# Channel layer norm of the convolution branch: block sums on VectorE ahead of one all-ones product, in place of eight products

## The reference, cut to what matters

```
a = a_val * sigmoid(a_glu)
y = depthwise_conv(a, width 31) + conv_b
mu = mean(y over the 1024 channels)
yc = y - mu
y = yc * rsqrt(mean(yc * yc over the 1024 channels) + eps) * cln_g + cln_b
ya = silu(y) * silu(a_z)
yb = windowed_attention(q, k, v) * silu(b_z)
h = h + concat(ya, yb) @ w_out
```

## Time and profile before

| | |
|---|---|
| median of three runs | 2235.05 us |
| profiled execution, first to last instruction (span) | 2231.8 us |
| TensorE matmul busy | 2197.3 us (98%) |
| TensorE weight load busy | 1929.3 us (86%) |
| VectorE busy | 1695.6 us (76%) |
| ScalarE busy | 1071.7 us (48%) |
| GpSimd busy | 546.4 us (24%) |
| mean granted TensorE clock | 0.998 |

### The profile page before, as it was taken

The page is one execution under the profiler, slowest core; times in us unless marked ns, Lnnn a source line. Parts: engine busy times, 40 slices in busy tenths (PEclk is TensorE's granted clock), DMA queues, the critical chain, the costliest instruction groups (busy, mean ns, idle before and its releaser), DMA issues.

```text
span 2231.8 us, 38880 instructions
## 1 busy us (share of the span) xinstructions
PE 2197.3 (98%) x14626; PEld 1929.3 (86%) x14626; DVE 1695.6 (76%) x2875; ACT 1071.7 (48%) x1429; POOL 546.4 (24%) x225
## 2 busy tenths in 40 slices
PE   7999999999999999999999999999999999999997
PEld 6888888888888888899999887888888888888886
DVE  7688678885888588788888666788888884447887
ACT  5445464445454464555554644444444443334454
POOL 4676641017767530110001322200000000000001
PEclk9999999999999999999999999999999999999999
DMA  7454445555554445554445300555555555555554
GB/s 254 169 181 169 155 170 179 188 185 197 177 181 165 144 178 187 187 193 166 165 157 194 114 3 21 192 186 188 187 188 188 188 188 188 188 188 189 188 209 168
DMA packets 69320, 384.89 MB, mean 172 GB/s; under 512 B 15120, under 2 KB 23056, under 8 KB 24272
## 3 DMA queue, kind: packets, MB, share of 16 engines
q1 hardware_dynamic: 69200, 383.22, 48.8%
HBM read 380.02 MB, written 3.18 MB: 172 GB/s over the span
## 4 chain that ended last, share of the span: by engine, by line
PE 92%; DVE 4%; ACT 1%; DMA 1%; issue 1%; POOL 0%; SPq 0%; DVEq 0%; POOLq 0%; ACTq 0%
PE ps L259 47%; PE ps L260 25%; PE ps L262 3%; PE ps L247 3%; PE ps L249 2%; PE ps L248 2%; PE ps L886 1%; DVE low L234 1%; PE ps L867 1%; DMA raw<-weights_dram 1%; PE ps L875 1%; PE ps L1882 1%; PE ps L1934 0%; PE ps L1926 0%; ACT whi L229 0%
## 5 line engine op out<-in xcount | busy, mean ns | idle before, releaser
L259 PE MATMUL ps<-opA,whi 128*128 128x512 f32 x2460 | 871.9, 395 | 0.3 <-DVE low L234 0.3
L260 PE MATMUL ps<-opA,low 128*128 128x256 f32 x2624 | 706.7, 279 | 0.2 <-DVE opA L1004 0.2
L229 ACT ACTIVATE whi<-raw 128x2048 fp32r<-128x2048 f32 x346 | 660.2, 1909 | 77.4 <-DMA raw<-weights_dram 76.2
L234 DVE TENSOR_TENSOR low<-raw,whi 128x2048 fp32r<-128x2048 f32 x252 | 583.3, 2315 | 67.8 <-ACT whi L229 52.2
L259 PEld LDWEIGHTS ps<-opA,whi 128*128 128x128 f32 x2460 | 461.0, 187 | 106.2 <-issue 2.8
L241 POOL TENSOR_TENSOR low<-raw,whi 128x2048 fp32r<-128x2048 f32 x95 | 436.6, 4606 | 433.6 <-ACT whi L229 407.2
L259 PE MATMUL ps<-opB,whi 128*128 128x512 f32 x1380 | 494.5, 398 | 14.9 <-DVE opB L418 12.1
L260 PEld LDWEIGHTS ps<-opA,low 128*128 128x128 f32 x2624 | 492.0, 188 | 14.3 <-DVE opA L1004 0.5
L260 PE MATMUL ps<-opB,low 128*128 128x256 f32 x1472 | 397.3, 280 | 0.0
L259 PEld LDWEIGHTS ps<-opB,whi 128*128 128x128 f32 x1380 | 259.7, 188 | 78.1 <-DVE low L412 10.5
L268 ACT ACTIVATE crossed<-ps 128x256 f32<-128x256 f32 x168 | 64.6, 384 | 490.6 <-PE ps L262 490.4
(11 more groups left out here) (399 smaller groups left out, 2660.9 us busy)
## 6 DMA issues: line engine op xcount, KB each, us to landing
raw<-weights_dram SPq DMA_DIRECT2D x350, 1024.0 KB, 4.8
bias_t<-table_dram SPq DMA_DIRECT2D x16, 384.0 KB, 6.0
hT<-xT_dram SPq DMA_DIRECT2D x4, 512.0 KB, 9.0
out_dram<-hT SPq DMA_DIRECT2D x3, 512.0 KB, 2.8
lora_g<-lora_dram SPq DMA_DIRECT2D x1, 1024.0 KB, 5.1
p_in<-pT_dram SPq DMA_DIRECT2D x2, 256.0 KB, 5.2
lora_wa<-lora_dram SPq DMA_DIRECT2D x1, 512.0 KB, 5.5
chunk_mats_dram<-compact SPq DMA_DIRECT2D x4, 128.0 KB, 3.9
```

Source lines behind the costliest of these rows:

```text
L229: act.activation(whi[:, v % RING, :], raw[:, v % RING, :], ACT.Copy).then_inc(hi_done.sem, 1)
L234: v_.tensor_tensor(wlo(v % RING, 0, width), raw[:, v % RING, 0:width], whi[:, v % RING, 0:width].bitcast(F32), ALU.subtract).then_inc(lo_d ...
L259: pe.matmul(*cross, start=start, stop=False)
L260: mm = pe.matmul(ps[:, b, 0:T], wlo(s, w0, w0 + P), op[:, k, 0:T], start=False, stop=False)
```

## The change

The seven sums of y_ln's blocks, and three sums of y_sq (four blocks onto four, two onto two, one onto one), are done by VectorE; TensorE then does one all-ones product for the mean and one for the variance. y_sq grows to eight blocks and its second half now lies on bias_t, so ScalarE's second square waits until VectorE has read the last rows of bias_t (biased(8), in step 38), and both squares stand in step 38 ahead of ScalarE's gate(38). The sum y_sum takes p_in's place.

```diff
-        y_sq = place("y_sq", [P, 4, T], at=arena + 1088)
+        y_sq = place("y_sq", [P, 8, T], at=arena + 1088)
+        y_sum = place("y_sum", [P, T], at=arena + 11528)
...
                     if m == 38:
                         act.wait_ge(*fr["centred"](1))
-                        act.activation(y_sq[:, :, :], y_ln[:, 0:4, :], ACT.Square).then_inc(fr["y_sq"].sem, 1)
-                    if m == 39:
-                        act.wait_ge(*fr["var_mm"](1))
-                        act.activation(y_sq[:, :, :], y_ln[:, 4:8, :], ACT.Square).then_inc(fr["y_sq"].sem, 1)
+                        act.activation(y_sq[:, 0:4, :], y_ln[:, 0:4, :], ACT.Square).then_inc(fr["y_sq"].sem, 1)
+                        act.wait_ge(*fr["biased"](PAIRS))
+                        act.activation(y_sq[:, 4:8, :], y_ln[:, 4:8, :], ACT.Square).then_inc(fr["y_sq"].sem, 1)
...
                         else:
-                            ins = v.scalar_tensor_tensor(y_ln[:, cc, :], taps, w, y, ALU.mult, ALU.add)
-                            if cc == CB - 1:
-                                ins.then_inc(fr["conv"].sem, 1)
-                                v.wait_ge(*fr["conv"](1))
-                            else:
-                                link(ins)
+                            link(v.scalar_tensor_tensor(y_ln[:, cc, :], taps, w, y, ALU.mult, ALU.add))
+                            if cc:
+                                ins = v.tensor_tensor(y_sum[:, :], y_ln[:, 0, :] if cc == 1 else y_sum[:, :], y_ln[:, cc, :], ALU.add)
+                                if cc == CB - 1:
+                                    ins.then_inc(fr["y_sum"].sem, 1)
+                                else:
+                                    link(ins)
...
+                    if m == 38:
+                        v.wait_ge(*fr["y_sq"](2))
+                        for x in (4, 2):
+                            link(v.tensor_tensor(y_sq[:, 0:x, :], y_sq[:, 0:x, :], y_sq[:, x:2 * x, :], ALU.add))
+                        v.tensor_tensor(y_sq[:, 0, :], y_sq[:, 0, :], y_sq[:, 1, :], ALU.add).then_inc(fr["sq_sum"].sem, 1)
                     if m == 39:
-                        v.wait_ge(*fr["var_mm"](2))
+                        v.wait_ge(*fr["var_mm"](1))
...
-                def variance(x):
-                    pe.wait_ge(*fr["y_sq"](x + 1))
-                    for c in range(4):
-                        mm = pe.matmul(ps[:, 5, T:2 * T], ones[:, :], y_sq[:, c, :], start=x == 0 and c == 0, stop=x == 1 and c == 3)
-                    mm.then_inc(fr["var_mm"].sem, 1)
+                def variance():
+                    pe.wait_ge(*fr["sq_sum"](1))
+                    pe.matmul(ps[:, 5, T:2 * T], ones[:, :], y_sq[:, 0, :], start=True, stop=True).then_inc(fr["var_mm"].sem, 1)
...
                 def mean():
-                    pe.wait_ge(*fr["conv"](1))
-                    for c in range(CB):
-                        mm = pe.matmul(ps[:, 5, 0:T], ones[:, :], y_ln[:, c, :], start=c == 0, stop=c == CB - 1)
-                    mm.then_inc(fr["mean"].sem, 1)
+                    pe.wait_ge(*fr["y_sum"](1))
+                    pe.matmul(ps[:, 5, 0:T], ones[:, :], y_sum[:, :], start=True, stop=True).then_inc(fr["mean"].sem, 1)
...
-                    if m in (38, 39):
-                        variance(m - 38)
+                    if m == 39:
+                        variance()
```

More of the change, by code:

```diff
@@ L481, in program @@
         att_keysT = [place(f"keysT{x}", [P, KV_HEADS, T], at=area + x * KB * 2 * T + 8 * P) for x in range(2)]
-        fr_counts = {"flip_in": 16, "p_in": 16, "p_hi": 1, "p_lo": 1, "gate": 24, "gated": 24, "conv": 1,
+        fr_counts = {"flip_in": 16, "p_in": 16, "p_hi": 1, "p_lo": 1, "gate": 24, "gated": 24,
                      "tok": 1, "tok_read": 1, "turned": 1, "v_read": 1, "k_read": 1,
@@ L485, in program @@
                      "out": 8, "normed": 8, "outT": 8, "mixed": 8, "hi": 8, "lo": 8,
-                     "mean": 1, "centred": 1, "y_sq": 2, "var_mm": 2, "var": 1, "dev": 1, "inv": 1, "scaled": 1,
+                     "mean": 1, "centred": 1, "y_sq": 2, "y_sum": 1, "sq_sum": 1, "var_mm": 1, "var": 1, "dev": 1, "inv": 1, "scaled": 1,
                      "affine": 8, "th": 8, "once": 8, "w": 8, "w_hi": 8, "w_lo": 8,
```

## The result

| | before | after |
|---|---|---|
| median, same chip | 2234.91 us (4 runs) | **2265.35 us** (2262.70 to 2267.57, 4 runs) |
| profiled execution: span, own time | 2231.8 us | 2263.4 us, 2265.39 us |
| TensorE matmul, busy | 98% | 97% |
| VectorE busy | 1695.6 us | 1755.9 us |
| GpSimd busy | 546.4 us | 545.9 us |

The change makes the kernel slower: ratio 1.0137, 95% interval 1.0123 to 1.0150. That is 30.4 us more, where 21.2 were forecast. TensorE has 14 products fewer in each layer and yet lost.

What follows compares the result with a forecast made beforehand. TensorE was taken to set the front's pace; 8.6 us a layer, 17.2 for both, plus 4 us of clock on the 2231.8 us span gave 2253.0, and 3.25 us outside it 2256.3 us; 80% range 2240 to 2272.

Steps and rivals of the forecast that it cites:

- Products removed: Layer norm on TensorE: 14 of 16 all-ones products go, at 0.43 us each, 6.0 us a layer saved.
- The row that decides: VectorE beside GpSimd splits: a two-SBUF-input operation waits for the split's end; the engine that has waited is served next.
- blocked sum: VectorE block sum beside a GpSimd split: ends 0.28 us after the split, making VectorE 3.67 us late.
- GpSimd's keeping its turn: Rival, paired splits: the second split precedes the waiting sum, VectorE 8.2 us late, +27.3 us a layer, some 2311 us; 12%.
- the absence of blocking: Rival, sums beside splits: each costs its plain 0.42 us, -4.3 us a layer, 2226.4 us; 8%.
- Blocks 1 to 6: Block sums in the groups: 0.1 us for block 1, then 1.07 us in each of five groups, 5.35 us.
- The mean: Block 7's sum at step 35: held by a split, TensorE starts at 259.22 instead of 255.58, 3.64 us.
- The variance: Sums of squares: the split goes ahead of the third sum, TensorE waits 5.5 us; 1.2 us if unblocked.
- A layer in all: One layer's sum of terms: 0.1 + 5.35 + 3.64 + 5.5 - 6.0 = +8.6 us; +17.2 us for both.
- The clock: TensorE's clock after the mean and variance waits: one fall a layer at 2.0 us, +4 us, bounds 0 and 8.
- The 3.25 us outside the span: Outside first and last instruction: median of runs lies 3.25 us above the profiled span, where nothing changes.

Runs made afterwards that it cites:

- the products alone: Against the kernel before: one product for the mean, one for the variance, no VectorE sums, the other blocks left out of the computation; 2223.57 us (0.9949).
- fills: Changed kernel plus unread products in TensorE's waits: in groups, at mean and variance, 2260.37 us; at mean and variance only, 2257.65 us.
- the second experiment: Changed kernel with the three sums of squares replaced by one reduction over eight blocks, block sums as changed; 2255.73 us (1.0100 to the kernel before).
- the first experiment: Changed kernel with the running sum of the blocks kept in PSUM, sums of squares as changed; 2238.90 us (1.0023 to the kernel before).
- the third experiment: Changed kernel with both the running block sum in PSUM and one reduction for the squares; 2231.39 us (0.9993 to the kernel before).

## Why the forecast was right in sign and short in size

Step by step, by the forecast's own terms (layer 0 of the profiled execution, falls of the clock taken out):

- **Products removed, 6.0 us a layer:** right, 6.06 and 6.12 with the products alone.
- **The row that decides** (two SBUF inputs and a split exclude each other; the engine that waited is served): right. The forecast's blocked sum is 3.67 us, the median 3.672. GpSimd's keeping its turn did not happen in any of the twelve sums that had a second split behind the first (block 7 has none), and the absence of blocking in none of the fourteen.
- **Blocks 1 to 6:** 5.45 us forecast. From the start of the first group to that of the last block (83.75 to 250.19, before 83.84 to 242.77) it is 7.51 us; the one group with a fall has 6.89 us between two evictions where the others have 5.34, 1.55 us. Left: 5.96, as 1.15 us a group instead of 1.07 and 0.2 for block 1.
- **The mean:** 3.64 us forecast; 11.02 - 7.42 = 3.6 from the shifts of TensorE's product (255.58 to 266.60) and of L694 ahead of it (242.77 to 250.19).
- **The variance:** wait 5.5 us forecast, 5.25 measured; with fills 0.36.
- **A layer in all:** 8.6 us forecast. 15.35 - 1.55 - 4.9 = 8.9 in layer 0; in layer 1, where a group has a fall of about the same 1.55 us, 14.3 - 1.55 - 3.8 = 8.95. Both layers together 17.9 instead of 17.2.
- **The clock: the term that failed.** I counted one fall a layer at 2.0 us, 4 us, with 8 as the upper bound. Measured: three a layer, 1.55 + 4.9 and 1.55 + 3.8, 11.8 us in the fronts. One of the three falls behind a wait of 0.9 or 1.1 us in a group, which the forecast had priced at nothing. Placing a wait "nearer" to 1.60 or to 10.49 by its ratio was a guess between two rows, and the rows were too far apart to carry it: 3.5 us at the mean gave a fall in both layers here and in only one of two in the second experiment, and even 0.93 us gave one once. The 2.0 us for one fall was near: 1.9 to 2.45 us at the mean and the variance (half of what the two cost together), 1.55 in a group.
- **The 3.25 us outside the span** were 2.0: the profiled execution after has 2265.39 us for a span of 2263.4. The forecast took the distance between a median of other executions and this span for a constant, and so hid 1.3 us of its error.

Against the span the forecast was 2253.0 us and the measurement 2263.4: 10.4 us, of which 7.8 are the falls in the fronts (11.8 - 4), 0.7 the waits and products there, and 1.9 the net of what lies behind the fronts: 1.2 for the longer wait of the second block and 1.5 for the fall behind it, less 0.8 that came back ahead of it in places that were not traced. The forecast had nothing for that last part, and no edit touches it.

What stays open: why eight of the forty waits of about 1 us in the groups (two of ten in the changed kernel, and one, two and three of ten in the three others that have them unfilled) dropped the clock and the others didn't, and why the wait of the second block was 2.73 us here and 1.52 before. It ends on ScalarE's rounding, which waits there for a load of weights, and it comes out long or short in kernels with quite different fronts.

## What to carry to other kernels

Before work is moved to VectorE, look at what GpSimd does at that moment and at where the operands lie: with two SBUF inputs a 0.42 us addition takes up to the rest of GpSimd's instruction, here 3.7 us, and a PSUM operand or another moment makes it 0.42 us again. A reduction with one SBUF input ran beside a split unharmed, but not every one-input operation does: the one on sinT in the earlier trace rows was held for 4.75 us. Idle time of an engine covers such a delay only once a group, and the idle time that is left decides, not the mean busy share. And price each new wait of TensorE twice, once for itself and once for the clock: here the late sums cost 18 us beyond the 12 us of products that they saved, and the falls of the clock in the fronts 12 us more.

## What the runs showed of the hardware beyond that

- **An engine that has waited is served between two instructions of the other that stand back to back.** GpSimd's pair of splits took 9.32 us with a sum in the middle and 9.16 without, although the second split was ready; the other eleven such pairs took 9.30 or 9.31 us. At the variance it was GpSimd that had waited, and it went ahead of VectorE's third sum.
- **One wait, two outcomes.** The second block's wait, over all twelve kernels: seven had it at 1.40 to 1.99 us, with no window under 1.00 behind it; five at 2.73 to 2.94 us, each with a window at 0.66 to 0.79. At the start, 1.15 to 1.60 us left the clock alone, and 1.97 to 2.30 us brought it to 0.70 to 0.78 and cost 1.3 us. TensorE's timeline there in the first experiment, and the windows of the same kernel:

```profile
17.19 0.50 PE L259 MATMUL ps<-opB,whi 128*128 128x512 f32 x1 [2.02 <-DVE opB L418]
```

```profile
15.00:20.00 5.00, 2.98 (x11) 2.42 (x10) 4.91 (x9) 4.48 (x9) 0.00 (x0) 0.76 1.02 363
20.00:25.00 5.00, 5.00 (x27) 4.32 (x27) 4.85 (x4) 5.00 (x6) 0.00 (x0) 0.90 0.62 197
```

  Yet 1.99 us in one place had no fall and 1.97 us in the other had one, 0.93 us in a group had one, 2.5 us at the variance had one in layer 0 and none in layer 1 of the third experiment and one in both of the second, and 3.56 us at the mean had none there in layer 0. A wait of 1.55 us at 1262 to 1305 us, the same in all twelve kernels, had a window at 0.71 or 0.72 behind it in two of them. The length of the wait alone doesn't settle it.
- **A reduction over 128x2048 in one operation (3.83 us) does what sums of 1024, 512 and 256 columns do in 1.94 + 0.42 us of plain time,** so it is the slower form, and it is the better one only where a split would stop the last sum.
